# Who adds the gathered value rows: one stage table of a two-layer mixture-of-experts trunk is emptied but for one row

## The reference

```python
def peer_ffn(h, w_q, sub_keys, u, v):
    ...
        q = (xb @ w_q).reshape(BLK, PEER_HEADS, PEER_QDIM)
        ...                                   # top 16 by 2 x 128 sub-keys, for each of 8 heads
        e = jnp.take_along_axis(i1, ci // K, axis=-1) * PEER_N_KEYS + jnp.take_along_axis(i2, ci % K, axis=-1)
        g = jax.nn.softmax(sc, axis=-1)
        ue = u[e]
        ve = v[e]
        a = jax.nn.gelu(jnp.einsum('thkd,td->thk', ue, xb).astype(jnp.float32), approximate=False) * g
        return jnp.einsum('thk,thkd->td', a.astype(xb.dtype), ve)
```

## Time and profile before

| what | us |
|---|---|
| median of 3 runs | 2897.97 |
| profiled execution | 2902.58 |
| its span | 2900.4 |
| TensorE busy | 2284.9 |
| VectorE busy | 2184.6 |
| ScalarE busy | 1183.7 |
| TensorE matmuls of the picks (L1723) | 1542.5 |
| VectorE dots (L1094) | 1235.4 |
| VectorE side additions (L1085) | 346.0 |

### The profile page before, as it was taken

How to read it: one execution, slowest core, us unless ns; L and a number is a source line. 1 busy time by engine, 2 the same in 40 slices (tenths; PEclk the granted TensorE clock), 3 DMA queues, 4 the chain that set the end, 5 groups by cost and what they waited for, 6 DMA issues and landing times.

```text
span 2900.4 us, 27200 instructions
## 1 busy us (share of the span) xinstructions
PE 2284.9 (79%) x7394; PEld 1213.3 (42%) x7394; DVE 2184.6 (75%) x5166; ACT 1183.7 (41%) x3457; POOL 1244.1 (43%) x1049
## 2 busy tenths in 40 slices
PE   9779787788877887786887878877788878886567
PEld 8536442454424554243443434443354434432122
DVE  2688678876878757796688876988679876887664
ACT  3154334344343443445344453435534453433333
POOL 0254335443444333444434543354434444345655
PEclk9899999899999898998899988989889998988989
DMA  6599999999999999999999999999999999999998
GB/s 271 209 418 421 398 398 416 421 421 403 415 420 421 420 375 420 420 418 421 421 393 406 422 421 420 389 416 421 421 402 406 421 421 421 399 421 421 422 422 350
DMA packets 170817, 1170.27 MB, mean 403 GB/s; under 512 B 19668, under 2 KB 19928, under 8 KB 36136
## 3 DMA queue, kind: packets, MB, share of 16 engines
q0 software_dynamic: 147456, 1073.81, 89.7%
q1 hardware_dynamic: 23208, 94.74, 8.3%
HBM read 1164.28 MB, written 4.19 MB: 403 GB/s over the span
## 4 chain that ended last, share of the span: by engine, by line
DMA 28%; DVE 14%; PE 11%; issue 6%; POOL 3%; ACT 3%; POOLq 0%; DVEq 0%; ACTq 0%
DMA ring<-in_uv,pick 26%; PE acc L1723 6%; DVE ring L1094 4%; POOL ring L666 3%; PE ps L1514 3%; DVE side L1085 1%; DMA xc<-h 1%; DMA stream<-in_strips 1%; ACT diag L1368 1%; DVE arena L969 1%; DVE arena L950 1%; DVE arena L1040 1%; DVE arena L1044 1%; DVE arena L951 1%; DVE arena L1031 1%
## 5 line engine op out<-in xcount | busy, mean ns | idle before, releaser
L666 POOL DMA_INDIRECT ring<-in_uv,pick x1024 | 1239.7, 1211 | 1630.5 <-PE acc L1723 1092.9
L1723 PE MATMUL acc<-ring,diag 128*128 128x512 f32 x2988 | 1542.5, 659 | 465.3 <-ACT diag L1368 462.3
L1094 DVE CUSTOM_DVE_ANT_0 ring<-ring,h_now 128x1024 f32<-128x1024 f32 x1024 | 1235.4, 1222 | 490.2 <-DMA ring<-in_uv,pick 474.0
L1723 PEld LDWEIGHTS acc<-ring,diag 128*128 128x128 f32 x2988 | 582.6, 207 | 1287.7 <-ACT diag L1368 702.8
L1357 ACT ACTIVATE gelu<-dots 128x1 f32<-128x1 f32 x1024 | 206.1, 201 | 1264.6 <-DVE dots L1094 1258.0
L1085 DVE SCALAR_TENSOR_TENSOR side<-ring,coef,side 128x1024 f32<-128x1024 f32 x270 | 346.0, 1281 | 23.1 <-ACT coef L1360 23.0
L1360 ACT ACTIVATE coef<-gate,gelu 128x1 f32<-128x1 f32 x1024 | 302.0, 295 | 33.2
L1368 ACT ACTIVATE diag<-ident,coef 128x128 f32<-128x128 f32 x747 | 300.1, 402 | 29.8 <-PE acc L1723 5.5
L1514 PE MATMUL ps<-resident,actT 128*128 128x256 f32 x896 | 220.3, 403 | 14.5 <-ACT actT L1169 14.5
L1514 PEld LDWEIGHTS ps<-resident,actT 128*128 128x128 f32 x896 | 178.1, 202 | 58.9 <-issue 18.2
L1481 PE MATMUL ps<-actT,stream 128*128 128x128 f32 x960 | 124.9, 291 | 23.6 <-DMA stream<-in_strips 22.7
(11 more groups left out here) (198 smaller groups left out, 1454.6 us busy)
## 6 DMA issues: line engine op xcount, KB each, us to landing
stream<-in_strips SPq DMA_DIRECT2D x102, 512.0 KB
resident<-in_strips SPq DMA_DIRECT2D x18, 1024.0 KB, 12.9
ring<-in_uv,pick POOLq DMA_INDIRECT x1024
ring<-in_strips SPq DMA_DIRECT2D x9, 1024.0 KB, 19.6
arena<-in_keys SPq DMA_DIRECT2D x8, 512.0 KB
xc<-in_x SPq DMA_DIRECT2D x4, 512.0 KB
h<-arena SPq DMA_DIRECT2D x4, 512.0 KB, 11.4
xc<-h SPq DMA_DIRECT2D x4, 512.0 KB
```

The lines of the kernel that those rows point to most:

```text
L666: pool.indirect_dma_start(ring[:, n % SLOTS, :], None, tables[layer], bass.IndirectOffsetOnAxis(ap=pick[:, col:col + 1], axis=0),).then_in ...
L1094: dve.tensor_tensor_reduce(ring[:, slot, 0:D], ring[:, slot, 0:D], h_now[:], 1.0, 0.0, ALU.mult, ALU.add, dots[:, slot:slot + 1]).then_inc ...
L1723: m = pe.matmul(acc[:, b * 512:(b + 1) * 512], diag[:, turn % 4, :], ring[:, slot, D + b * 512:D + (b + 1) * 512], start=(r == 0 and i == ...
```

## The change

The "swa" line of `VECTOR` keeps one entry: round 0, place 1, whose addition starts `side` from the residual. In stages 3 to 7 the other 33 rows of a stage go to TensorE, with a `diag` by ScalarE for each.

```diff
-    "swa": (
-        ((1, 4, 7),) * 2 + ((0, 2, 4, 6),) + ((0, 4),) + ((1, 5),) + ((0, 3, 6),) + ((2, 6),) +
-        ((1, 4, 7),) * 2 + ((2, 6),) + ((1, 3, 5, 7),) + ((0, 3, 6),) + ((),) * 4),
+    "swa": ((1,),) + ((),) * 15,
```

## The result

The changed kernel takes 2916.97 us, the median of 4 runs (2915.5 to 2922.09), against 2898.02 of 4 runs of the kernel before: ratio 1.0068, 95% interval 1.0052 to 1.0084. In a later set of runs it was 2916.41 against 2899.29, ratio 1.006 (1.0045 to 1.0075). It is slower by 17 to 20 us. The profiled execution took 2915.5 us with a span of 2913.8, 13.4 more than the span before. The two traces can account for these 13.4 us only: the profiled execution of the kernel before, 2902.58 us, was 4.6 us over its median, and that of the changed kernel 1.5 us under its own.

A forecast was written before the change was run, and what follows sets the result against it. DMA gathers were taken to bound the kernel; 17 us lost around the query and `kv` strips, less 2 before expert choice, gave +15: a median of 2913 us from 2898.0, forecast 2904 to 2922 (chance 0.50), range 2897 to 2932.

The forecast's parts named there:

- What bounds: Whole kernel: DMA gathers at about 421 GB/s set the cadence; a late engine costs nothing until the issued gathers run dry.
- Stretch one: Stages 3 to 6, query and `kv` strips: added picks delay `kv` and gather 34, so the DMA idles; 17 us in all.
- The squares and `qvar` behind the late `kv`: Behind `kv`: ScalarE's squares and VectorE's `qvar` some 6 us later each, picks catch up before their slots; nothing added.
- Stretch two: Output strips to expert choice: five picks hidden at full clock, `x2` chain 1 us earlier a stage; -2 us for four stages.
- The last stage: Last stage: DMA already full and TensorE quick enough at full clock, so the change there is 0.
- the early term: The cost around the query and `kv` strips of stages 3 to 6, 17 us.
- the late term: The gain from output strips to expert choice, -2 us for four stages.
- The wait before gather 34: Sign in the changed trace: POOL waits over 10 us before issuing gather 34.
- The last sign of a wrong forecast: Rounds 12 to 15 losing less than now by over 2 us a stage would show the forecast wrong.
- A: Rival, chance 0.25: the ring's queue covers the delay; early cost 4, later gain 4, so 2898 us within 5.
- B: Rival, chance 0.09: relieved VectorE and fuller clock shorten expert choice by 3 us in each of four stages; 2889 us.
- C: Rival, chance 0.16: TensorE becomes the bound through much of stages 3 to 6; a middle of +30, 2928 us.

The follow-up runs named there:

- the two complementary tables: Against the kernel before: rounds 0 to 3 kept and 22 rows a stage moved, 0.9991; rounds 0 to 3 moved (11 rows) and the rest kept, 1.0044.
- the halved strips: The changed kernel with every other product over k left out of the second layer's query and `kv` strips: 2900.7 us, 1.0004 to the kernel before.
- Its own experiment: The kernel before with only rounds 10 and 11 of stages 3 to 7 emptied, 7 rows a stage: 2899.01 us, ratio 0.9989.
- the second execution: A second profiled execution of the changed kernel, with nothing else altered: 2916.01 us, span 2914.3.
- The first experiment: Against the kernel before, rounds 0 to 3 of stages 3 to 7 kept, the 22 rows of rounds 4 to 11 moved to TensorE: 2898.8 us, ratio 0.9991.
- the experiment: The kernel before with the changed table in the last stage only, stages 3 to 6 as before: 2898.06 us, ratio 0.9993.
- the two-row experiment: The changed kernel with picks 18 and 20 of each stage kept on VectorE, 31 of 33 rows moved: 2904.81 us, 1.0019 to the kernel before.
- the control: The kernel before with every other product over k left out of the second layer's query and `kv` strips: 2901.75 us, ratio 1.0013.

## Why the prediction was right, step by step

**What bounds.** Right. The ring's queue of gathers decides: the time follows the GB/s in every run above; 212 us less of VectorE and 204 more of TensorE's busy time moved the span by 13.4.

**Stretch one.** The mechanism and its place were right, and shown by the two complementary tables (0.9991 and 1.0044) and the halved strips (1.0004). The working held closely in stage 4: 57.4 us from the run to the end of `kv` (57.5 predicted), gather 34 issued 60.1 us behind the run's start (59.8; a gather follows the end of its pick by 0.95 us in stage 4 of both traces, not 0.6). Its size was 17 us; the DMA windows have 23 and 22. This term was too small.

Part of what was missing can be seen. I looked at gather 34 alone; the DMA runs short 20 us earlier. First a window of the kernel before, then four of the changed kernel in stage 4:

```profile
1621.00:1626.00 5.00, 5.00 (x19) 3.25 (x18) 4.34 (x8) 1.19 (x4) 2.33 (x2) 1.00 1.01 423
...
1623.00:1628.00 5.00, 5.00 (x14) 2.24 (x13) 3.17 (x7) 4.40 (x9) 2.67 (x4) 1.00 0.89 264
1628.00:1633.00 5.00, 5.00 (x20) 3.48 (x19) 4.56 (x9) 1.11 (x5) 1.43 (x1) 1.00 0.94 372
1633.00:1638.00 5.00, 5.00 (x16) 2.55 (x15) 1.23 (x2) 1.18 (x2) 3.61 (x3) 1.00 0.93 338
...
1643.00:1648.00 5.00, 5.00 (x13) 2.17 (x12) 4.83 (x12) 4.77 (x13) 4.38 (x3) 1.00 0.89 316
```

POOL issues gather 27 at 1622.44 after 4.60 us of waiting, and its dot starts at 1631.43, 9 us behind the issue, where the median in the page after is 14.0 to the landing alone. So the lateness is spread over several gathers, and the predicted wait of over 10 us before gather 34 didn't come: it was 5.05. Counted on the cadence, though, the lateness of gather 34 holds that of the gathers ahead of it. The prediction's own sum on the rows of the changed kernel (the dot of pick 22 at 1264.57, 1614.55, 1958.31 and 2301.14, the issue of gather 34 at 1290.69, 1643.00, 1985.87 and 2328.78 in stages 3 to 6) makes it 3.2, 5.5, 4.7 and 4.7 us late, 18 in all. In stage 4 that is all that the windows show (5.5); in the others the windows have 1.5 to 2.2 us more; where that comes from isn't settled. The 6.97 us from an issue to its dot is no floor: the changed trace has 6.10 (pick 13 of stage 5, 1928.45 to 1934.55), by which the sum would be smaller still. The order of the stages came out: stage 3 least (4.9 us in the windows), the others 5.5 to 6.8, against 2.3 and 4.7 to 5.2.

**The squares and `qvar` behind the late `kv`.** Nothing speaks against adding nothing: gather 41 of stage 4 has to wait 3.04 us and is issued at 1657.28, by the same cadence 2.4 us late, less than the 5.5 by which gather 34 had already held the DMA up. No run took it apart.

**Stretch two.** Predicted -2. Its own experiment has about -3, weakly; the late windows of the changed kernel give 8 us (6.7 in the second execution), more than the term allowed for. That TensorE would be at full clock there was right: 0.97 to 0.99 granted in these windows, 0.93 to 0.97 before. `h2T` starts at 1806.23 in stage 4, 8.7 us behind the gain's end and without a wait, so the five picks cost what was worked out; before, it waited 1.02 us for VectorE. Where the 8 us come from can be narrowed down. These are the late windows of the run that moved only rounds 0 to 3 and so has the late table of before:

```profile
1448.00:1565.00 117.00, 99.45 (x363) 53.77 (x361) 102.87 (x334) 49.55 (x140) 48.35 (x43) 0.98 1.01 411
1793.00:1911.00 118.00, 101.40 (x361) 54.95 (x360) 103.10 (x335) 49.22 (x139) 47.18 (x42) 0.95 1.00 402
2139.00:2256.00 117.00, 99.69 (x358) 53.94 (x358) 101.01 (x330) 49.09 (x138) 45.84 (x42) 0.96 0.98 400
2481.00:2600.00 119.00, 103.04 (x363) 55.22 (x361) 103.34 (x337) 49.73 (x141) 48.80 (x43) 0.94 1.00 405
```

Against 398, 401, 400 and 408 before, that is some 3 us less lost, nearly all in stage 3, with no late row moved. The first experiment, with no early row moved, has 398, 408, 404 and 407, also some 3 us. So part of the 8 is likely a give-back of the early loss, which the prediction said could not be ("nothing later gives DMA time back"), and part goes with the late rows. Each is one execution and hardly more than a window's error, so the split is indicated, not shown; and whether the late part is the fuller clock, slots that come free sooner because no addition waits for the next dot, or the chain of `x2` was not taken apart.

**The last stage.** Predicted 0. The stage is 2.2 us shorter in the trace (319.1, not the "still 322" that was named as a sign), and the experiment has no change that can be told. Small either way.

**The sum.** The +15 came from 17 - 2 + 0; the trace has 23 - 8 - 1.5. Two terms were mis-sized by 6 us each in opposite directions, so it is luck that the total came out as near as it did. The mechanism and place of the early term and the signs of both were no luck; that of the late term isn't shown.

**The signs.** `kv` was 11.8 us further behind `hT` (12 predicted), the DMA slices fell to 390 to 393 in all four stages, and the attention part had a granted clock of 0.99. The wait before gather 34 and the 322 us were missed. The last sign of a wrong forecast, late rounds that lose less than now by over 2 us a stage, was met in stages 3 to 5 by the windows from round 11 on (3.6, 2.5 and 2.2 us): it points at the late term, as above.

**The rivals.** A (the queue covers it) would have needed 5 to 7 us a stage more of spare; the two-row experiment, which takes 3.5 us from the backlog and brings back two thirds of the loss, shows how close it was. B (faster) is in the sign of the late terms alone. C (TensorE the bound) fell with the first experiment: TensorE was busy for 125.15 of the 137 us from 1645 to 1782, at a granted clock of 0.99, and the DMA still moved 421 GB/s.

## What to carry to other kernels

Where a DMA queue limits and everything else hides behind it, a shift of work between engines is priced not by its total but by the one stretch in which the receiving engine falls further behind than the queue is deep: here 12 picks and 5 strips in a time that the DMA needs for 12 picks. Sum the receiving engine's work over that stretch, compare the last release in it with the time at which its slot's next transfer is due, and count only the excess. That sum gave 17 to 18 us where the DMA lost 22 to 23, and it gives nothing for what comes back later, so it finds the place better than the size. Here two rows in that stretch were worth about 12 us, and 22 rows elsewhere nothing or 3 us the other way.

## What the runs showed of the hardware that was not expected

In these runs TensorE was granted more clock, the more rows it had: 0.915 before, 0.924 with 11 rows a stage added (in five stages), 0.944 with 22 and 0.955 with 33, and in the last stage 0.99 for 0.88, with 504 matmuls in place of 373 in the window. The 131 added matmuls cost 38 us of busy time there, 0.29 us each, where one takes 0.43 from start to start at full clock.

In the control, halving 20 strips' products made the kernel slower by 0.13% (0.04 to 0.23) rather than equal. The granted clock of its profiled execution, 0.912, is a little under the 0.915 of the kernel before. Whether this is the cause wasn't tried, and so small a difference may also be none.
